# A tenth buffer for the first expert pieces, from a smaller descriptor scratch and dead tables, and two gathers and a selection moved from the fifth to the sixth group

## The chip, the core and the metric

The kernel runs on one core of a Trainium2 chip. The time is what the device takes for one execution, in microseconds (us), and less is better. The engines are TensorE (PE in the profile; PEld is its weight load), VectorE (DVE), ScalarE (ACT), GpSimd (POOL) and SyncE (SP), which here only issues DMAs. Each of them runs its own list of instructions in order and waits on semaphores for the others. DMAs that SP issues stand in one queue (q1, "hardware_dynamic"), those that POOL issues in another (q0, "software_dynamic"); both are served by the same 16 DMA engines.

## The reference, cut to what matters

One sequence of 256 tokens of width 1024 passes through two blocks. The first block is a mixer (an mLSTM and a latent attention, each with a branch projection, gated, merged and projected out) and then a mixture of experts; the second is a sparse attention mixer and a gated feed-forward layer with a short convolution. The change is in the mixture of experts and just ahead of it. Its core is this:

```python
in_grp = jnp.take_along_axis(e_logits, grp[:, None, None], axis=1)[:, 0]
top_p, top_e = lax.top_k(jax.nn.softmax(in_grp, axis=-1), TOP_K)
weights = p_grp[:, None] * top_p / jnp.sum(top_p, axis=-1, keepdims=True)
...
def run_block(args):
    xb, e, wb = args
    a = jax.nn.silu(xb @ w_gate[e]) * (xb @ w_up[e])
    return (a @ w_down[e]) * wb[:, None].astype(xb.dtype)
```

There are 32 experts. Each token is sent to two of them, chosen by a router (first one group of four, then the best two of its eight experts), and the two results are added with the router's weights. w_gate and w_up are 1024x256 and w_down is 256x1024 for each expert, all float32, so all experts together are 100.7 MB of weights.

## The kernel before, in words

**The groups.** The experts are taken four at a time, one on each quarter of the 128 partitions of the result, with room for 32 tokens each. Eight groups (numbers 0 to 7) cover the 32 experts once. Experts with more than 32 tokens get further blocks of 32: four "later" groups (numbers 8 to 11) with 15 blocks in all, whose experts are known only once the router is done. The order in which the groups are worked is `ORDER = [0, 1, 2, 8, 3, 9, 4, 5, 10, 6, 11, 7]`; `o` in the code is a position in it, `g` a group.

**The pieces.** The weights of a group of four experts come as six pieces of 2 MB, numbered 6g to 6g+5. Pieces 0 to 3 of a group hold gate and up columns and are used by `gate_up` (line 1347, 16 matmuls a piece), pieces 4 and 5 hold the down weights and are used by `down_rows` (line 1423, 16 matmuls a piece). SP issues the pieces in order (only piece 3, whose buffer comes free late, follows piece 7). For the first nine (`SLOTS = 9`) there are nine buffers made of whatever memory is free by then: four in `big`, one in `dring`, two in `ring`, one put together from `hT`, `gateb` and `pT`, and one from `xs` and `tail`. The list `FIRST` says which piece goes into which. From piece 9 on, the four buffers in `big` are used in turn (`RING = 4`), with one exception: piece `ONCE = SLOTS + RING = 13` goes into `dring`. SP issues a piece when the piece that was in its buffer before has been used; PE counts `s_used` up by one for each piece used. Beside this, `ring`, `dring`, `xs` and `tail` go over to the later groups.

**The later groups.** Their weights come in three parts each (two for gate and up, used by `later_gate_up`, line 1362; one for down, used by `later_down_rows`, line 1438). (8, 0) is the first part of group 8, (8, 2) its down part. POOL fetches each part with up to four indirect DMAs of 1 MB, one per block, whose row numbers come from the router (`later_piece`, line 2313). Blocks that no expert needs have row numbers out of range, and such rows are skipped. With these inputs one block is needed, group 8's first (all of POOL's queue moves 3.17 MB, three parts of one block); the DMAs of the other 14 are issued all the same. Parts alternate between two buffers: even numbers in `ring`, odd ones in `dring`, `xs` and `tail`. Part number 0, (8, 0), waits until the first pieces in `ring` are used (`s_used` at 8, that is piece 7). Part number 1, (8, 1), waits until `dring` is free, that is until piece 13 is used. Part number n from 2 on waits until part n-2 is used (`s_lused` at n-1). Where PE uses a part is written in three tables: `AFTER` (behind a group's first piece), `INSIDE` (behind its fourth) and `BEHIND` (after its down projection).

**Gathers and selections.** The tokens of two positions in `ORDER` (a pair q) are gathered by PE from the token rows with a 0/1 matrix that POOL builds (`select_pair`, lines 2292 and 2300): four `gather` calls per pair (line 1304, 8 matmuls each), each of which needs a PSUM bank that DVE and ACT must have emptied. Afterwards `selects` (lines 1314 and 1316) turns that matrix for the way back and takes out each row's weight; POOL may then build the next pair's matrix (it waits on `s_stw`). `scatter` (line 1374) adds the outputs of a position to the sum over all experts. `hidden_columns` (line 1396) turns the hidden activations ahead of the down projection. In group 4 the third and fourth gather of pair 4 and the selection of pair 4 stand between `hidden_columns` and the down projection.

**Ahead of the experts.** SP loads the mixer's last projections (`ba0`, `ba1`, `bm0`, `bm1`, `out0`, `out1`, 2 MB each in four quarters, line 640) as the quarters before them are used, and then the first pieces. `s_mt2` reaches 4 when the turned mLSTM output has been written, after the latent attention. `filler` (line 895) are matmuls on zeros whose result nobody reads.

## Time and profile before

| | us |
|---|---|
| median of 3 runs | 1025.64 |
| lowest and highest of the 3 | 1022.02, 1027.52 |
| the profiled execution's own time | 1023.9 |
| its span in the trace | 1022.1 |
| PE busy | 972.6 (95%) |
| PEld busy | 713.1 (70%) |
| DVE, ACT, POOL busy | 492.0, 385.7, 379.7 |

The span is cut into 40 slices of 25.6 us in the page. The experts run from about 350 us to about 571 us, slices 14 to 22. The page's DMA row has 9 (90% or more) in every slice from 13 to 20 and 8 in the next three; its GB/s row has 360 to 427 there. PE has 8 or 9 in each of these slices. So two resources are close to full in this stage, and a wait of one of them decides it only for stretches of a few microseconds. Times in the rows below are microseconds from the span's start. `[1.01 <-DMA big<-in_pieces_dram]` behind a row of the timeline says that the engine sat idle for 1.01 us before it and that this DMA ended the wait; "issue" says that nothing that the profile shows ended it.

### The profile page before, as it was taken

Reading aid. Unit: us, or ns where it says so; the run is one execution under the profiler, and the core shown is the slowest. Engines: PE = TensorE matmul, PEld = TensorE weight load, DVE = VectorE, ACT = ScalarE, POOL = GpSimd, SP = SyncE. Lnnn points to the kernel's source line nnn. Section 1 sums busy time; section 2 is a strip of 40 time slices with the busy share of each in tenths; the row PEclk is TensorE's granted clock in tenths of the full one; section 3 lists DMA queues with packets and bytes.
Section 4 is the critical chain, followed back from the end, with each engine's and each line's share of the span. In section 5 each row is a group of like instructions: output and inputs, shape, how many; then the busy total and the mean of one; then the engine's idle time right before and its main releaser. Section 6 shows DMA issues by size and latency. Waiting matters only on the chain.

```text
span 1022.1 us, 15203 instructions
## 1 busy us (share of the span) xinstructions
PE 972.6 (95%) x6120; PEld 713.1 (70%) x6120; DVE 492.0 (48%) x853; ACT 385.7 (38%) x617; POOL 379.7 (37%) x249
## 2 busy tenths in 40 slices
PE   7999999999999999898699999999999999999997
PEld 3887777777788544344243699777556789999996
DVE  1445358544244622213031603536665368777775
ACT  1633345445433321111020644544553254434342
POOL 0885747444783055453320499740002500000000
PEclk7999999999999999999799999999999999999999
DMA  9996955334469999999999888533224465454521
GB/s 377 345 414 266 372 172 158 87 100 124 144 208 427 360 425 423 416 398 370 407 407 414 310 321 255 156 93 103 86 80 144 165 268 195 176 204 165 205 82 41
DMA packets 49274, 252.08 MB, mean 247 GB/s; under 512 B 10432, under 2 KB 11072, under 8 KB 31424
## 3 DMA queue, kind: packets, MB, share of 16 engines
q1 hardware_dynamic: 42736, 248.10, 64.4%
q0 software_dynamic: 6480, 3.17, 1.1%
q8 instruction: 41, 0.67, 0.3%
q14 instruction: 17, 0.14, 0.0%
HBM read 294.22 MB, written 1.05 MB: 289 GB/s over the span
## 4 chain that ended last, share of the span: by engine, by line
PE 76%; DVE 7%; issue 6%; DMA 4%; ACT 3%; POOL 2%; DVEq 0%; SPq 0%; POOLq 0%; ACTq 0%
PE ps L885 33%; PE ps L1208 17%; PE ps L1347 3%; PE ps L781 2%; PE ps L1423 2%; PE ps L1362 2%; PE ps L1374 2%; PE ps L833 1%; PE ps L1304 1%; DMA tail<-in_experts_dram,xidx 1%; PE ps L1438 1%; DMA big<-in_pieces_dram 1%; DMA xs<-in_x_dram 1%; PE ps L895 1%; POOL sel L2292 1%
## 5 line engine op out<-in xcount | busy, mean ns | idle before, releaser
L2262 POOL TENSOR_TENSOR wl<-ring,wh 128x1024 fp32r<-128x1024 f32 (+5 forms) x132 | 289.3, 2211 | 228.9 <-ACT wh L1760 227.1
L1760 ACT ACTIVATE wh<-ring 128x1024 fp32r<-128x1024 f32 (+5 forms) x148 | 143.4, 983 | 132.1 <-PE ps L885 100.9
L885 PE MATMUL ps<-wh,hTh 128*128 128x512 f32 (+3 forms) x384 | 153.0, 398 | 1.3 <-DVE wl L3086 1.3
L885 PE MATMUL ps<-wl,hTh 128*128 128x512 f32 (+3 forms) x384 | 148.3, 386 | 0.0
L885 PE MATMUL ps<-wh,hTl 128*128 128x512 f32 (+3 forms) x352 | 136.7, 388 | 0.0
L1208 PE MATMUL ps<-hTs,wsp 128*128 128x256 f32 x1056 | 128.7, 284 | 0.5 <-DVE wsp L2922 0.5
L1208 PEld LDWEIGHTS ps<-hTs,wsp 128*128 128x128 f32 x1056 | 128.1, 192 | 1.5 <-DVE wsp L2922 0.7
L2250 POOL TENSOR_TENSOR small<-small 128x2 f32<-128x2 f32 (+2 forms) x7 | 5.3, 759 | 272.7 <-DVE small L3235 192.4
L885 PEld LDWEIGHTS ps<-wh,hTh 128*128 128x128 f32 x384 | 73.0, 190 | 22.7 <-issue 6.8
L885 PEld LDWEIGHTS ps<-wl,hTh 128*128 128x128 f32 x384 | 73.0, 190 | 13.5
L885 PEld LDWEIGHTS ps<-wh,hTl 128*128 128x128 f32 x352 | 66.8, 190 | 13.4
L1208 PE MATMUL ps<-wsp,aTs 128*128 128x512 f32 x264 | 61.7, 391 | 0.0
L1347 PE MATMUL ps<-big,xg 128*32 128x512 f32 x432 | 53.7, 605 | 7.3 <-DMA big<-in_pieces_dram 7.0
L885 PE MATMUL ps<-hTh,wh 128*128 128x256 f32 x208 | 58.1, 279 | 0.0
L885 PE MATMUL ps<-hTl,wh 128*128 128x256 f32 x208 | 58.0, 279 | 0.0
L885 PE MATMUL ps<-hTh,wl 128*128 128x256 f32 x208 | 57.6, 277 | 0.0
L1976 ACT ACTIVATE wsp<-ring 128x2048 fp32r<-128x2048 f32 x22 | 42.0, 1909 | 40.4 <-PE ps L1208 34.1
L1208 PEld LDWEIGHTS ps<-wsp,aTs 128*128 128x128 f32 x264 | 49.0, 188 | 9.7
L2922 DVE TENSOR_TENSOR wsp<-ring,wsp 128x2048 fp32r<-128x2048 f32 x22 | 50.3, 2285 | 9.5 <-ACT wsp L1976 9.5
L2292 POOL TENSOR_SCALAR sel<-cst,few 128x128 fp32r<-128x128 f32 x40 | 23.3, 596 | 58.6 <-PE ps L1316 58.6
L885 PEld LDWEIGHTS ps<-hTh,wh 128*128 128x128 f32 x208 | 39.1, 188 | 0.8 <-issue 0.8
L885 PEld LDWEIGHTS ps<-hTl,wh 128*128 128x128 f32 x208 | 39.1, 188 | 0.0
(481 smaller groups left out, 1637.3 us busy)
## 6 DMA issues: line engine op xcount, KB each, us to landing
big<-in_pieces_dram SPq DMA_DIRECT2D x42, 2048.0 KB
ring<-in_wa_dram SPq DMA_DIRECT2D x68, 512.0 KB, 3.9
big<-in_mod_dram SPq DMA_DIRECT2D x11, 2048.0 KB, 10.4
ring<-in_ffn_dram SPq DMA_DIRECT2D x11, 2048.0 KB, 9.1
ring<-in_wb_dram SPq DMA_DIRECT2D x40, 512.0 KB, 3.9
dring<-in_ffn_dram SPq DMA_DIRECT2D x11, 1024.0 KB, 4.9
ring<-in_wb_dram SPq DMA_DIRECT2D x12, 384.0 KB, 5.7
dring<-in_pieces_dram SPq DMA_DIRECT2D x2, 2048.0 KB, 21.4
```

The costliest lines, as they stand in the source:

```text
L781: mm = pe.matmul(ps[32 * q:32 * q + 32, 6, :], condw[:, c, :], mtile[n][:, c, :], start=(c < 4), stop=(c >= 4), skip_group_check=True)
L885: mm = pe.matmul(out, x[i], y[j], start=(p, c, k) == (0, 0, 0), stop=(c, k) == (KD - 1, 2), skip_group_check=True)
L1208: mm = pe.matmul(out, w[a], x[b], start=start and n == 0, stop=stop and n == 2, skip_group_check=skip)
L1347: mm = pe.matmul(ps[b * BS:(b + 1) * BS, 4, :], xg[q % 2][:, c, at:at + BS], slot_part(s, b)[:, cc * 512:(cc + 1) * 512], start=(c == 0), ...
L1362: mm = pe.matmul(ps[b * BS:(b + 1) * BS, 5, :], xg[q % 2][:, c, at:at + BS], later_slot(later_number(g, k), b)[:, cc * 512:(cc + 1) * 512] ...
L1374: mm = pe.matmul(ps[:, 2 * t + n, :], selT[:, (o // 2) % 2, o % 2, t * P:(t + 1) * P], x[:, n * 512:(n + 1) * 512], start=False, stop=Fals ...
L1423: mm = pe.matmul(ps[b * BS:(b + 1) * BS, 6 + n, :], aT[:, f, b * BS:(b + 1) * BS], slot_part(s, b)[:, n * 512:(n + 1) * 512], start=(f == ...
L1760: nc.scalar.activation(quarter(name, q, "high"), quarter(name, q, "raw"), ACT.Copy).then_inc(s_qh, 1)
L1976: nc.scalar.activation(wsp[:, 0 if last else m, 0, :], src, ACT.Copy).then_inc(s_hi[m], 1)
L2262: nc.gpsimd.tensor_tensor(quarter(name, q, "low"), quarter(name, q, "raw"), quarter(name, q, "high"), ALU.subtract).then_inc(s_ql, 1)
L2292: ins = nc.gpsimd.tensor_scalar(sel12[:, k, t, h * P:(h + 1) * P], const("iota"), gsp[:, k, t, g:g + 1], None, ALU.is_equal)
L2922: V.tensor_tensor(wsp[:, dst, 1, :], src, wsp[:, dst, 0, :], ALU.subtract).then_inc(s_lo[m], 1)
```

## The change

There is one more buffer for first pieces, number 9: three blocks of new memory (`tenth`, 12 KB a partition) and a fourth in the tables `cos`, `sin`, `chunk` and `tri`, which nobody reads after the latent attention. The memory comes from a descriptor scratch of 4096 bytes a partition in place of the default of 16384. To make the tables adjoin, `tri` is moved behind `chunk` and its bfloat16 copy is made earlier, in memory of its own; the zeros for `filler` become 480 columns wide.

Piece 0 goes into the new buffer and is issued between `bm0` and `bm1` once `s_mt2` is at 4. The other first pieces each move up by one place, so that ten pieces are loaded ahead of the ring. With `SLOTS` at 10, `ONCE` becomes 14: piece 14 is the one that goes into `dring`, part (8, 1) therefore waits for piece 14, and part (8, 0) waits for `s_used` at 9, that is piece 8. On PE part (8, 0) moves from inside group 2 to behind group 1. The third and fourth gather of pair 4 move from group 4's end to behind the second and third piece of group 5, and the selection of pair 4 moves from group 4 to group 5. On POOL the matrix of pair 5, which waits for that selection, moves behind parts (10, 1) and (10, 2).

PE at the end of group 1 and the start of group 2, before (`_66` is the second buffer of gathered tokens; 32x512 rows are pieces or parts, 128x256 rows gathers):

```order
L1423 MATMUL ps<-big,aT 32x512 [waits s_piece2]
L1423 MATMUL ps<-big,aT 32x512 x7
L1347 MATMUL ps<-big,xg_66 32x512 [waits s_xa,s_piece3]
L1347 MATMUL ps<-big,xg_66 32x512 x7
L1347 MATMUL ps<-dring,xg_66 32x512 [waits s_xv,s_piece4]
L1347 MATMUL ps<-dring,xg_66 32x512 x7
```

and now:

```order
L1430 MATMUL ps<-big,aT 32x512 [waits s_piece1]
L1430 MATMUL ps<-big,aT 32x512 x7
L1369 MATMUL ps<-ring,xg_66 32x512 [waits s_xv,s_xa,s_later0]
L1369 MATMUL ps<-ring,xg_66 32x512 x15
L1354 MATMUL ps<-big,xg_66 32x512 [waits s_xa,s_piece2]
L1354 MATMUL ps<-big,xg_66 32x512 x7
```

Part (8, 0), in `ring` and with its wait on `s_later0`, has moved ahead of all of group 2.

POOL from part (9, 2) on, before (dring, xs and tail rows are odd parts, ring rows even ones):

```order
L2313 DMA dring<-in_experts_dram,xidx 128x2048 [waits s_lused]
L2313 DMA dring<-in_experts_dram,xidx 128x2048
L2313 DMA xs<-in_experts_dram,xidx 128x2048
L2313 DMA tail<-in_experts_dram,xidx 128x2048
L2313 DMA ring<-in_experts_dram,xidx 128x2048 [waits s_lused]
L2313 DMA ring<-in_experts_dram,xidx 128x2048 x3
L2292 TENSOR_SCALAR sel_81<-cst,few 128x128 [waits s_stw]
L2292 TENSOR_SCALAR sel_81<-cst,few 128x128 x7
L2300 TENSOR_TENSOR sel<-sel_81 128x512 [waits s_ga2,c_pool]
L2313 DMA dring<-in_experts_dram,xidx 128x2048 [waits s_lused]
```

and now from part (10, 0) on:

```order
L2320 DMA ring<-in_experts_dram,xidx 128x2048 [waits s_lused]
L2320 DMA ring<-in_experts_dram,xidx 128x2048 x3
L2320 DMA dring<-in_experts_dram,xidx 128x2048 [waits s_lused]
L2320 DMA dring<-in_experts_dram,xidx 128x2048
L2320 DMA xs<-in_experts_dram,xidx 128x2048
L2320 DMA tail<-in_experts_dram,xidx 128x2048
L2320 DMA ring<-in_experts_dram,xidx 128x2048 [waits s_lused]
L2320 DMA ring<-in_experts_dram,xidx 128x2048 x3
L2299 TENSOR_SCALAR sel_81<-cst,few 128x128 [waits s_stw]
L2299 TENSOR_SCALAR sel_81<-cst,few 128x128 x7
L2307 TENSOR_TENSOR sel<-sel_81 128x512 [waits s_ga2,c_pool]
```

The matrix of pair 5 (sel) no longer stands ahead of part (10, 1), the second group of dring rows.

The diff, without most of its context:

```diff
@@ -51,16 +51,16 @@
 NPIECE = 6
-SLOTS, RING = 9, 4
-FIRST = [0, 1, 2, 7, 3, 4, 5, 6, 8]
+SLOTS, RING = 10, 4
+FIRST = [9, 0, 1, 7, 2, 3, 4, 5, 6, 8]
-INSIDE = {2: (8, 0), 3: (9, 0), 4: (9, 2), 5: (10, 1), 6: (11, 0), 7: (11, 2)}
+INSIDE = {3: (9, 0), 4: (9, 2), 5: (10, 1), 6: (11, 0), 7: (11, 2)}
-BEHIND = {2: (8, 1)}
+BEHIND = {1: (8, 0), 2: (8, 1)}
-SELECTS = {0: 0, 1: 1, 2: 2, 4: 3, 6: 4, 9: 5}
+SELECTS = {0: 0, 1: 1, 2: 2, 4: 3, 7: 4, 9: 5}
@@ -75,7 +75,7 @@
 CONST, NCONST = columns([
-    ("ident", P), ("ones", P), ("tri", P), ("cos", T), ("sin", T), ("chunk", SPAN), ("causal", SPAN),
+    ("ident", P), ("ones", P), ("cos", T), ("sin", T), ("chunk", SPAN), ("tri", P), ("causal", SPAN),
@@ -189,9 +189,11 @@
         pT = sb("pT", 3, SPAN)
-        zero = sb("zero", 512, dt=BF16)
+        zero = sb("zero", 480, dt=BF16)
+        halves16 = sb("halves16", 2, P, dt=BF16)
+        tenth = sb("tenth", 3, PIECE // QUAD)
@@ -286,6 +288,8 @@
                 return xs[:, b, :] if b < 2 else tail[:, b - 2, :]
+            if s == 9:
+                return tenth[:, b, :] if b < 3 else cst[:, CONST0:CONST0 + PIECE // QUAD]
...
@@ -420,8 +426,7 @@
         assert wh1_at + 4 * 1792 <= cst_at + 4 * NCONST
-        tri16 = at("tri16", spare_at + 4 * 1024, P, dt=BF16)[:, :]
-        ones16 = at("ones16", spare_at + 4 * (1024 + P // 2), P, dt=BF16)[:, :]
+        tri16, ones16 = halves16[:, 0, :], halves16[:, 1, :]
@@ -456,7 +461,7 @@
         s_lg, s_re, s_rx, s_diff = (sem(n) for n in ("s_lg", "s_re", "s_rx", "s_diff"))
-        s_piece = [sem(f"s_piece{n}") for n in range(SLOTS)]
+        s_piece = [sem(f"s_piece{n}") for n in range(SLOTS - 1)] + s_mt[3:]
@@ -667,10 +672,6 @@
             mod_tile(11)
-            for name, _, _ in LOADS[8:]:
-                load(name, wa)
-
-
@@ -678,6 +679,8 @@
                     sp.wait_ge(s_used, slot_before(n) + 1)
+                elif s == 9:
+                    sp.wait_ge(s_mt2, KD // 2)
@@ -690,7 +693,7 @@
                 w = PIECE // 2
-                if s == 7:
+                if s in (7, 9):
@@ -701,7 +704,11 @@
                                  pieces[n].rearrange("h p n -> p h n")).then_inc(s_piece[s], 16)
-            for n in (0, 1, 2, 4, 5, 6, 7, 3, 8):
+            for name, _, _ in LOADS[8:]:
+                load(name, wa)
+                if name == "bm0":
+                    expert_piece(0)
+            for n in (1, 2, 4, 5, 6, 7, 8, 3, 9):
...
@@ -1324,7 +1331,7 @@
                 s = slot(n)
-                first = 48 if s == 7 else 32 if s == 8 else 16
+                first = {7: 48, 8: 32, 9: 16 * mod_count(3) + 48}.get(s, 16)
@@ -1481,6 +1488,8 @@
                         early_gather(q, k - 1)
+                    if g == 5 and k in (1, 2):
+                        early_gather(4, k + 1)
@@ -1491,8 +1500,6 @@
                     hidden_columns(o)
-                    early_gather(q, 2)
-                    early_gather(q, 3)
@@ -2056,6 +2063,8 @@
                     gathered(q, 0, 6)
+                if g == 5:
+                    gathered(4, 2, 6)
@@ -2070,8 +2079,6 @@
                     outputs_high(o - 1)
-                if g == 4:
-                    gathered(q, 2, 6)
@@ -2304,9 +2311,9 @@
                 if n == 0:
-                    pool.wait_ge(s_used, FIRST.index(6) + 1)
+                    pool.wait_ge(s_used, max(FIRST.index(5), FIRST.index(6)) + 1)
-                    pool.wait_ge(s_used, max(SLOTS, ONCE + 1))
+                    pool.wait_ge(s_used, ONCE + 1)
@@ -2327,9 +2334,9 @@
             later_piece(10, 0)
-            select_pair(5)
+            select_pair(5)
@@ -2531,6 +2538,8 @@
             link.n += 1
+            link.later(V.tensor_copy(tri16, const("tri")))
+            link.later(V.tensor_copy(ones16, const("ones")))
@@ -2713,8 +2722,6 @@
             part_mean(4)
-            link.later(V.tensor_copy(tri16, const("tri")))
-            link.later(V.tensor_copy(ones16, const("ones")))
@@ -2893,6 +2900,8 @@
                     gathered(q, 1, 7)
+                if g == 5:
+                    gathered(4, 3, 7)
@@ -2900,7 +2909,7 @@
                     outputs_low(o - 1)
-                if q:
+                if q and g != 4:
@@ -3394,7 +3403,7 @@
               "rows": np.ascontiguousarray(rows), "mod": mod, "wa": wa, "experts": experts, "pieces": pieces, "wb": wb, "ffn": ffn}
-    nc = bacc.Bacc("TRN2", target_bir_lowering=False, num_devices=1)
+    nc = bacc.Bacc("TRN2", target_bir_lowering=False, num_devices=1, dynamic_dma_scratch_size=4096)
```

## Rows read from the trace of the kernel before

**Rows 1.** Stretches: bounds, us; PE, PEld, DVE, ACT, POOL busy; PEclk, DMA share, GB/s.
```profile
344.00:350.00 6.00, 4.85 (x26) 2.90 (x28) 4.01 (x15) 1.19 (x3) 0.00 (x0) 1.00 0.56 184
...
484.00:510.00 26.00, 17.50 (x125) 5.51 (x118) 1.69 (x4) 1.04 (x3) 9.71 (x10) 0.80 1.02 421
...
520.00:560.00 40.00, 39.59 (x295) 17.46 (x290) 10.18 (x18) 6.70 (x13) 6.10 (x6) 1.00 1.02 424
```

**Rows 2.** Chain of waits, 345 to 520 us: start us, us, what.
```profile
365.32 3.43 PE ps L1347 x32
368.76 1.14 PE ps L1304 x8
369.90 1.85 PE ps L1347 x16
...
382.50 10.20 DMA big<-in_pieces_dram
...
396.75 3.57 PE ps L1362 x32
...
476.23 4.67 POOL sel L2292 x8
...
486.41 13.14 DMA tail<-in_experts_dram,xidx
```

**Rows 3.** Timeline of PE, groups 2 and 3: start us, us, operation.
```profile
383.95 1.93 PE L1347 MATMUL ps<-big,xg 128*32 128x512 f32 x16
...
392.74 1.92 PE L1347 MATMUL ps<-big,xg 128*32 128x512 f32 x16 [1.01 <-DMA big<-in_pieces_dram]
...
407.64 0.63 PE L1362 MATMUL ps<-dring,xg 128*32 128x512 f32 x2
...
412.61 1.92 PE L1347 MATMUL ps<-big,xg 128*32 128x512 f32 x16 [1.33 <-DMA big<-in_pieces_dram]
...
420.87 5.34 PE L1438 MATMUL ps<-ring,aT 128*32 128x512 f32 x32 [3.45 <-issue]
...
426.00 1.93 PE L1347 MATMUL ps<-big,xg 128*32 128x512 f32 x16
```

**Rows 4.** Waits of ACT, 262 to 303 us: total us, times, longest.
```profile
ACT wh L1760 <- PE ps L885: 28.7, 16, 3.3
```

**Rows 5.** Timeline of SP: the issue of piece 10.
```profile
354.73 0.38 SPq L701 DMA_DIRECT2D big<-in_pieces_dram  x1
```

**Rows 6.** Timeline of POOL: first DMA of (8, 0) and of (8, 1).
```profile
369.81 1.26 POOL L2313 DMA_INDIRECT ring<-in_experts_dram,xidx  x1 [2.87 <-issue]
...
388.42 1.09 POOL L2313 DMA_INDIRECT dring<-in_experts_dram,xidx  x1 [2.16 <-PE ps L1347]
```

**Rows 7.** Both DMA queues, 380 to 385 us: packets, MB, share.
```profile
q1 hardware_dynamic: 272, 2.10, 99.1%
q0 software_dynamic: 271, 0.00, 3.1%
```

**Rows 8.** POOL's queue, 374 to 389 and 393 to 406 us.
```profile
q0 software_dynamic: 576, 1.05, 18.2%
...
q0 software_dynamic: 571, 1.04, 20.8%
```

**Rows 9.** Timeline of PE, groups 4, 5 and 7.
```profile
470.94 0.39 PE L1304 MATMUL ps<-sel,hnh 128*128 128x256 f32 x1 [1.03 <-DVE olt L2860]
...
476.53 3.64 PE L1423 MATMUL ps<-big,aT 128*32 128x512 f32 x32 [0.41 <-ACT selT L2025]
...
479.96 0.63 PE L1347 MATMUL ps<-big,xg 128*32 128x512 f32 x2
...
492.38 2.80 PE L1347 MATMUL ps<-big,xg 128*32 128x512 f32 x16 [3.62 <-DMA big<-in_pieces_dram]
...
499.59 1.07 PE L1362 MATMUL ps<-dring,xg 128*32 128x512 f32 x2 [4.41 <-DMA tail<-in_experts_dram,xidx]
...
554.12 1.92 PE L1347 MATMUL ps<-big,xg 128*32 128x512 f32 x16
```

More of the change, by code:

```diff
@@ L303, in slot_tile @@
                 return ring[:, (NLAST + s - 5) % 2, 0:PIECE]
+            if s == 9:
+                return tenth[:, 0:2, :].rearrange("p t n -> p (t n)")
             if s == 8:
@@ L894, in filler @@
                 for _ in range(n):
-                    pe.matmul(ps[:, b, :], zero[:, 0:P], zero[:, :], start=True, stop=True, skip_group_check=True)
+                    pe.matmul(ps[:, b, 0:480], zero[:, 0:P], zero[:, :], start=True, stop=True, skip_group_check=True)
             pe.wait_ge(s_zero, 1)
```

## The prediction, made before the changed kernel was run

> **What bounds the kernel now.** I read the stretches first, then the chain of waits, then the timelines of PE, SP and POOL and the DMA queues where the change acts. In the expert stage two resources are nearly full: from 520 to 560 us PE is busy 39.6 of 40 us and the DMA share is 1.02 at 424 GB/s; from 484 to 510 us PE is busy only 17.5 of 26 us at a mean granted clock of 0.80, while DMA stays at 1.02 [rows 1]. A 2 MB piece (2.097 MB) takes 4.95 us at 424 GB/s. The DMA engines have one early hole, 344 to 350 us, share 0.56 [rows 1]: all first buffers are full and the experts haven't started. The chain leaves PE for 10.20 us of a piece's DMA at 382.50, and later passes through POOL's matrix at 476.23 and 13.14 us of an indirect DMA at 486.41 [rows 2]. PE's waits on pieces are 1.01 us at 392.74, 1.33 at 412.61 and 3.62 at 492.38; those at 420.87 (3.45, shown as "issue", just where the part in `ring` must have landed) and 499.59 (4.41) are for later parts [rows 3, 9]. So there are three bounds that take turns: the stream of pieces, POOL's queue of parts, and PE. A buffer more helps the first alone; I have to see what it does to the second.
>
> **The tenth buffer.** Piece 0's 2 MB leave the stretch after 302 us and go beside the mixer's last projections. ACT there waits on PE's matmuls only (28.7 us in 16 waits) and on no DMA [rows 4], so I cost piece 0 at nothing; if its 4.95 us of DMA delayed `bm1` past its use, it would cost up to that. The gain is a stream 4.95 us ahead. But the first ring piece now waits for piece 1, not piece 0: piece 10 was issued at 354.73 [rows 5], a gather and a piece (1.14 + 1.85 [rows 2]) after piece 9, so 2.99 us of the lead are idle DMA. Net lead: 1.95 us.
>
> **Part (8, 0).** It now waits for piece 8, a gather and a piece later than piece 7, so its first DMA moves from 369.81 [rows 6] to 372.80. Its 576 packets filled 374 to 389 us [rows 8]. In 380 to 385 us POOL's queue got 271 packets through and SP's 272 [rows 7]: one each in turn, though POOL's rows were out of range and moved nothing. So a part of four blocks takes 10.6 us (576 packets at 54 a us) while pieces flow, and 15 when one block has data, however little it moves. The Trainium skill's page DMA: Bandwidth & Descriptors, section Queues, rings and completion order, says the engines go round-robin between queue rows a packet at a time; by that rule alone (8, 0) costs its upper bound below, unless the piece queue is empty. The trace agrees with it (271 against 272).
> So (8, 0) would end near 391.6, and PE sees a part some 1.9 us after its last packet (419 to 420.87, an estimate from where the packets of (8, 2) stop): 393.5. Before, PE came to it at 396.75. Now it stands behind group 1, where PE arrives at 383.95 [rows 3]: a wait of up to 9.5 us that wasn't there. What shortens it: piece 15 can't be issued before piece 10 is used, at about 382.5 [rows 2], and pieces 10 to 14 plus 1.05 MB of real rows (2.5 us) keep the queue busy from about 355.7 for 27.2 us, to 382.9. Then POOL's packets pass alone, for perhaps a microsecond. Bounds 2 and 9.5 us; I take 5, in the middle. PE starts (8, 0) at 388.9 and, at 3.57 us [rows 2], group 2 at 392.5 in place of 383.95.
>
> **Part (8, 1).** It waits for piece 14 in place of 13. Piece 14 is used two pieces (3.43), a gather and a piece after group 2's start, at 392.5 + 6.4 = 398.9; 0.9 us later the first DMA is issued, at 399.8 against 388.42 [rows 6]. Before, PE used the part at 407.64 [rows 3], 19.2 us after its issue, with 571 packets between 393 and 406 [rows 8]. Now: 399.8 + 19.2 = 419.0. PE arrives sooner: from group 2's start to (8, 1) it took 407.64 - 383.95 = 23.7 us, less (8, 0) with 3.57 and the wait of 1.01, so 19.1: 411.6. **A new wait of 7.4 us.** This is the step I trust most, since it needs only the order of POOL's waits and one issue-to-use time. Bounds: 2 us, if an empty piece queue helps it, and 10.
>
> **Part (8, 2).** From (8, 1)'s start to (8, 2)'s end PE took 426.00 - 407.64 = 18.4 us, of which waits are 1.33 and 3.45 and 1.7 is matmuls at a lower clock (5.34 us for 32 against 3.64 in row 476.53) [rows 3, 9]. The rest is 11.9: 419.0 + 11.9 = 430.9 without any wait. (8, 2)'s packets come 13 us behind (8, 1)'s and would be in time for 432.3, where PE needs them at 427.3: up to 5.0, less if the queue runs dry, since piece 22 can't be issued before piece 18 is used. I take 2, and 1.7 for matmuls after the long wait at the half clock, as after the wait at 420.87. So (8, 2) ends at 434.6: **8.6 us later than 426.00.**
>
> **Group 4.** Two gathers, the wait of 1.03 us ahead of them and a selection leave the stretch from about 469.9 to 476.53 [rows 9]. That is 1.03, two gathers at 1.14 and about 1.3, 4.6 us, the upper bound. But scatter needs three copies of group 9's outputs by DVE and ACT, the first of which is the one the 1.03 us waited for, and the gathers covered the other two; at something over 1 us a copy I take 1.8, with 0 as the lower bound: **-1.8**.
>
> **Groups 5 to 7.** The gathers go where PE waited 3.62 us, and POOL no longer builds pair 5's matrix (4.67 us, started 476.23 [rows 2]) ahead of (10, 1), whose wait of 4.41 us at 499.59 goes, with 0.9 us of slow matmuls (2.80 against 1.92). That makes 8.9 us on PE. But the piece stream is late next: piece 33 is used 492.38 - 479.96 = 12.4 us after group 4's end, and twelve more pieces at 4.95 follow, 59.4: piece 45 at 71.8 us, where it was 554.12 - 479.96 = 74.2 [rows 9]. PE's own work from piece 33 on is 554.12 - 492.38 = 61.7, less 4.41 and 0.9, plus an estimated 1.3 for the moved selection, 57.7 us against the stream's 59.4, so the stream sets it: **-2.4**. After piece 45 nothing changes.
>
> **Fillers.** 32 columns fewer, 13 ns a matmul at the full clock; only the 20 between the last pieces could be on the path: -0.3. The copies of `tri` and `ones` and the 64 KB that change DMA: nothing, DVE is at 48% on the page.
>
> **Sum.** 8.6 - 1.8 - 2.4 - 0.3 = +4.1 us on the profiled execution's 1023.9 (span 1022.1 and 1.8 around it): 1028.0. That execution lies 1.7 us below the median of 1025.64, so I predict 1025.6 + 4.1 = 1029.7, slower by 0.4%. The lead of 1.95 us from the tenth buffer isn't in the sum: once PE waits at (8, 1), the ring of four is full anyway.
>
> **Rival 1, the parts at full price (slower).** The piece queue never runs dry under the parts. Then (8, 0) costs 9.5 (4.5 more) and (8, 2) costs 5.0 (3.0 more): 1029.7 + 7.5 = 1037.2. For it: POOL's packets kept to one in turn for as long as pieces flowed [rows 7]. Against it: SP's queue is only four pieces deep and PE stands still. It decides from where (8, 0) is used later than 391 us.
>
> **Rival 2, the lead wins (faster).** Parts slip through in the holes that the waits make: (8, 0) costs 2 and (8, 1) about the same, and both are made up before 426 by the waits of 1.01, 1.33 and 3.45 that go. What stays is the lead of 1.95, the 1.8, the 2.4 and 0.3: 1025.6 - 6.4 = 1019.2. For it: the share of 0.56 at 344 us shows that the stream could start earlier, and PE's waits on pieces are real. Against it: (8, 1)'s issue depends on piece 14, which nothing brings forward.
>
> **Rival 3, no difference.** The stream of pieces has the same length and the ring is four deep either way; a delay of PE near 410 us is absorbed by the 3.62 and 4.41 near 495. Time 1025.6. The waits near 495 add up to enough (8.0 us), but the stream bound above leaves only 2.4 of them. Whether the smaller scratch slows POOL the trace of before can't show; its DMA rows wait on PE or on nothing that the profile shows [rows 6]. If POOL had to wait for room at every part, the time would be rival 1's, and it is in that chance.
>
> **Chances and range.** The forecast 0.43, rival 1 0.20, rival 2 0.25, rival 3 0.12. About 0.5% (5.1 us, from 1020.5 to 1030.8) is what a measurement of this kernel can tell from no change. The forecast's own range is 1026 to 1033, so 0.4 of it lies above 1030.8: slower 0.17 + 0.20 = 0.37. Faster is 0.8 of rival 2: 0.20. The same: the rest, 0.43. The range over the cases, with about a tenth left out on either side, is 1019 to 1036.
>
> **What would show it.** In the profile after: PE idle ahead of the first part behind group 1 (near 384 us, 2 to 9 us) and, longer, ahead of the part behind group 2 (near 411 us, 5 to 10 us), both ended by an indirect DMA; POOL's first `dring` DMA near 400 in place of 388; a granted clock below 1 just behind; group 5's fourth piece with a wait under 2 us, and none for the part behind it; DMA share near 1 from 490 to 560. I am wrong if PE runs through behind group 2 without a wait, or if group 3's first piece starts before 415 us. The step most likely to be mis-sized is the wait for (8, 0).

## The result, and the profile after

The changed kernel takes 1029.97 us (median of 9 runs, 1027.0 to 1032.36) against 1023.5 us (9 runs, 1019.75 to 1027.52) for the kernel before on the same chip: ratio 1.0069, 95% interval 1.0051 to 1.0087, so slower by 0.7%. The profiled execution has a span of 1028.9 us, 6.8 more than before. The difference arises in the expert stage. Its first expert matmul starts 1.46 us earlier (348.29 against 349.75), its last gate and up piece (piece 45) 6.75 us later. (On the page of the kernel before, the DMA row has its 9 up to slice 21, and PE's row has a 6, not 8 or 9, in slice 19, about 486 to 511 us, where the waits of 3.62 and 4.41 us lie.)

PE's timeline of the changed kernel, groups 1 to 3 (start us, us, operation; L1354, L1369, L1430, L1445 are L1347, L1362, L1423, L1438 of before), answers to [rows 3]:

```profile
384.75 5.34 PE L1369 MATMUL ps<-ring,xg 128*32 128x512 f32 x32 [2.03 <-DMA ring<-in_experts_dram,xidx]
...
394.59 1.92 PE L1354 MATMUL ps<-dring,xg 128*32 128x512 f32 x16
...
416.57 1.07 PE L1369 MATMUL ps<-dring,xg 128*32 128x512 f32 x2 [7.65 <-DMA tail<-in_experts_dram,xidx]
...
421.58 1.89 PE L1354 MATMUL ps<-big,xg 128*32 128x512 f32 x16
...
428.72 4.23 PE L1445 MATMUL ps<-ring,aT 128*32 128x512 f32 x32
432.77 1.89 PE L1354 MATMUL ps<-big,xg 128*32 128x512 f32 x16
```

PE stands 2.03 us for (8, 0), then works on it for 5.34 us in place of 3.57, and stands 7.65 us for (8, 1). Piece 19 starts at 432.77, where it was 426.00. POOL's timeline and its queue say why (8, 1) is late:

```profile
371.36 1.26 POOL L2320 DMA_INDIRECT ring<-in_experts_dram,xidx  x1 [5.86 <-issue]
...
397.34 1.09 POOL L2320 DMA_INDIRECT dring<-in_experts_dram,xidx  x1 [12.55 <-PE ps L1354]
```

POOL stood 12.55 us until PE had used piece 14 (the `dring` row at 394.59), and PE got the part 19.2 us after its issue, exactly as before (388.42 to 407.64 [rows 3, 6]).

What follows is new. Stretches 426 to 438 us (the columns of [rows 1]; the seventh value is the granted clock, then DMA share and GB/s), the kernel before and the changed one:

```profile
426.00:438.00 12.00, 12.00 (x104) 5.96 (x100) 5.34 (x8) 3.48 (x6) 4.12 (x4) 1.00 1.02 417
```

```profile
426.00:438.00 12.00, 12.00 (x83) 4.72 (x82) 3.17 (x3) 2.08 (x3) 4.57 (x6) 0.86 0.57 203
...
474.00:484.00 10.00, 7.79 (x38) 3.54 (x29) 2.51 (x2) 1.43 (x2) 3.56 (x3) 0.69 1.02 412
...
480.00:490.00 10.00, 9.07 (x60) 3.95 (x64) 2.51 (x2) 1.28 (x2) 4.58 (x4) 0.83 0.74 265
```

The DMA share of 0.57 in place of 1.02 is a hole of 12 x 0.45 / 1.02 = 5.3 us in the stream. The ring of four was full and piece 23 may only be issued once PE has used piece 19, which PE did 6.8 us late. So PE's wait has become lost time of the other full resource. It is the largest hole, not the only one: the share is 0.83 from 450 to 460 us and 0.74 from 480 to 490, where the kernel before has 1.02 and 0.97.

Groups 4 to 7 of the changed kernel, against [rows 9]:

```profile
473.01 0.62 PE L1445 MATMUL ps<-dring,aT 128*32 128x512 f32 x2 [2.72 <-issue]
...
480.93 1.84 PE L1381 MATMUL ps<-oh__67,selT 128*128 128x512 f32 x4 [2.21 <-ACT oh__67 L2039]
482.57 1.91 PE L1381 MATMUL ps<-ol__69,selT 128*128 128x512 f32 x4
484.41 3.69 PE L1430 MATMUL ps<-big,aT 128*32 128x512 f32 x32
487.93 1.89 PE L1354 MATMUL ps<-big,xg 128*32 128x512 f32 x16
...
499.04 1.92 PE L1354 MATMUL ps<-big,xg 128*32 128x512 f32 x16
500.78 0.60 PE L1369 MATMUL ps<-dring,xg 128*32 128x512 f32 x2
...
515.34 3.57 PE L1354 MATMUL ps<-big,xg 128*32 128x512 f32 x16 [3.07 <-DMA big<-in_pieces_dram]
...
560.87 1.92 PE L1354 MATMUL ps<-big,xg 128*32 128x512 f32 x16 [0.30 <-DMA big<-in_pieces_dram]
```

The waits of 3.62 and 4.41 us near 495 are gone: PE is 8.0 us late at 487.93 and only 1.2 at (10, 1) (500.78 against 499.59). But that isn't kept. The pieces are late too, PE waits for them (3.07 us at 515.34) and is again 6.75 us late at the last one. At 515.34 it is 4.0 us late (511.36 before), and the rest comes piece by piece behind it. A bound that PE had caught up with was not the one that counts.

### The profile page after: what moved, and what is told of

The parts are those of the page before. It is cut to its first block, busy times and chain, and to the rows that moved or that the text cites. A ratio compares the mean times of both kernels' runs of the same rounds, so it can differ in the third digit from the quotient of the medians.

```text
span 1028.9 us, 15205 instructions
## 1 busy us (share of the span) xinstructions
PE 975.4 (95%) x6120; PEld 712.1 (69%) x6120; DVE 495.3 (48%) x853; ACT 385.5 (37%) x617; POOL 380.7 (37%) x249
## 3 DMA queue, kind: packets, MB, share of 16 engines
q0 software_dynamic: 6480, 3.17, 1.1%
## 4 chain that ended last, share of the span: by engine, by line
PE 76%; DMA 8%; DVE 8%; issue 3%; ACT 3%; POOL 1%; DVEq 0%; SPq 0%; POOLq 0%; ACTq 0%
PE ps L892 32%; PE ps L1215 17%; DMA big<-in_pieces_dram 4%; PE ps L1354 4%; PE ps L1369 2%; PE ps L788 2%; PE ps L1381 2%; PE ps L1430 2%; PE ps L1445 2%; PE ps L1311 2%; DMA tail<-in_experts_dram,xidx 1%; PE ps L840 1%; DMA xs<-in_x_dram 1%; DMA ring<-in_experts_dram,xidx 1%; PE ps L1119 1%
## 5 line engine op out<-in xcount | busy, mean ns | idle before, releaser
L1215 PE MATMUL ps<-wsp,aTs 128*128 128x512 f32 x264 | 61.7, 390 | 0.0
L1354 PE MATMUL ps<-big,xg 128*32 128x512 f32 x400 | 49.4, 614 | 6.4 <-DMA big<-in_pieces_dram 6.4
L892 PEld LDWEIGHTS ps<-hTh,wl 128*128 128x128 f32 x208 | 39.6, 190 | 0.0
```

Source lines behind the costliest of these rows:

```text
L892: mm = pe.matmul(out, x[i], y[j], start=(p, c, k) == (0, 0, 0), stop=(c, k) == (KD - 1, 2), skip_group_check=True)
L1215: mm = pe.matmul(out, w[a], x[b], start=start and n == 0, stop=stop and n == 2, skip_group_check=skip)
L1354: mm = pe.matmul(ps[b * BS:(b + 1) * BS, 4, :], xg[q % 2][:, c, at:at + BS], slot_part(s, b)[:, cc * 512:(cc + 1) * 512], start=(c == 0), ...
```

## The experiments

In the table, "stage" runs from PE's first expert matmul to the start of piece 45, in the profiled execution (before 204.4, changed 212.6). "Idle" is how long the DMA engines stood in it: over the 20 stretches of 10 us from 350 to 550 us, the sum of 10 x (1.02 - share), where 1.02 is the share of a full queue (before 4.7, changed 13.5; good to a few tenths). Ratios are against the kernel before, run beside each, with 95% intervals.

| kernel | median us | ratio | stage us | idle us |
|---|---|---|---|---|
| changed, (8, 0) inside group 2 | 1023.53 | 1.0014 (0.9994 to 1.0034) | 206.5 | 8.0 |
| before, small scratch | 1023.77 | 1.0012 (0.9997 to 1.0026) | 202.7 | 2.9 |
| before, moved gathers | 1020.44 | 0.9972 (0.9956 to 0.9988) | 202.0 | 3.5 |
| changed, gathers not moved | 1030.5 | 1.0054 (1.0031 to 1.0078) | 212.1 | 13.7 |
| changed, piece 13 in dring | 1026.59 | 1.0030 (1.0013 to 1.0047) | 208.9 | 9.8 |
| the first and the fifth together | 1020.31 | 0.9979 (0.9963 to 0.9996) | 202.9 | 4.4 |
| changed, one DMA a part | 1015.76 | 0.9925 (0.9911 to 0.9940) | 198.1 | 3.4 |
| before, one DMA a part | 1014.64 | 0.9919 (0.9904 to 0.9934) | 197.8 | 2.6 |
| before, moved gathers, piece 12 in dring | 1019.99 | 0.9968 (0.9949 to 0.9988) | 201.9 | 3.0 |
| before, (8, 0) behind group 1 | 1031.77 | 1.0080 (1.0059 to 1.0102) | 211.5 | 10.4 |
| changed, (8, 0) inside, piece 12 in dring | 1023.56 | 1.0012 (0.9990 to 1.0033) | 203.7 | 5.5 |
| sixth, big at its old position | 1019.74 | 0.9969 (0.9951 to 0.9986) | 201.2 | 5.5 |

Stage less idle is 198 to 201 us in every row with all DMAs and in both kernels of the comparison, except the last row (196). So what sets these kernels apart is for the most part how long the stream of pieces stood. In the two rows with one DMA a part it is 195.

**(8, 0) back inside group 2.**

```diff
-INSIDE = {3: (9, 0), 4: (9, 2), ...
+INSIDE = {2: (8, 0), 3: (9, 0), 4: (9, 2), ...
-BEHIND = {1: (8, 0), 2: (8, 1)}
+BEHIND = {2: (8, 1)}
```

> The changed kernel, with part (8, 0) back inside group 2 and all else as changed. Theory (the order of POOL's waits): the loss is the wait for part (8, 1), 7.65 us at 416.57, which is issued only when piece 14 is used. With (8, 0) behind piece 15 again, PE no longer stands 2.03 us and no longer works 5.34 us (1.7 of it for the half clock) ahead of group 2, so pieces 12 to 14 are used some 7 to 9 us earlier and POOL issues (8, 1) near 389 in place of 397.34, while PE arrives at it only some 3.7 us sooner. The wait for (8, 1) falls to 2 to 5 us, group 3's piece 18 starts at 416 to 418 in place of 421.58, and of the 6.5 us that the change costs 2 to 5 go: 1025 to 1028. Rival (the late dring alone): the place of (8, 0) doesn't matter, since the wait is for POOL's queue of packets; time within 1 us of the changed kernel, 1029 to 1031. Rival (late parts don't decide, the stream does): also 1029 to 1031, with less wait at (8, 1) and more at pieces behind.

1023.53 us: all of the loss but 0.1% goes, a little more than the theory gave. PE's wait for (8, 1) falls from 7.65 to

```profile
410.26 0.62 PE L1369 MATMUL ps<-dring,xg 128*32 128x512 f32 x2 [4.20 <-DMA tail<-in_experts_dram,xidx]
```

and the DMA share from 426 to 438 us rises from 0.57 to 0.78; piece 19 starts at 429.20, where it was 432.77. Both rivals (1029 to 1031) are out.

**The small scratch alone.**

```diff
-    nc = bacc.Bacc("TRN2", target_bir_lowering=False, num_devices=1)
+    nc = bacc.Bacc("TRN2", target_bir_lowering=False, num_devices=1, dynamic_dma_scratch_size=4096)
```

> The kernel before with a descriptor scratch of 4096 bytes a partition in place of the default, nothing else. Theory: POOL doesn't lack room for descriptors, so the time is that of the kernel before within 0.2% (1021.5 to 1025.5), and the issue of (8, 0) to its first packet stays near 4.4 us. Rival (the smaller scratch slows POOL's indirect DMAs): parts (8, 1), (8, 2) and (10, 1), on which PE waits already, come later, 3 to 8 us slower, 1027 to 1032, and this alone would be the loss of the change.

1023.77 us, ratio 1.0012 with an interval up to 1.0026. A loss of 3 us or more by the scratch is excluded, one of 1 to 2 us isn't; the stage of its profile is no longer than before.

**The moved gathers alone** (`SELECTS`, the two `early_gather` and `gathered`, and `select_pair(5)` as in the change, on the kernel before).

> The kernel before with only the third and fourth gather of pair 4 and its selection moved to group 5, and POOL's matrix of pair 5 behind (10, 1) and (10, 2); nine buffers and part (8, 0) inside group 2 as before. Theory: group 4 ends 1 to 3 us earlier, the wait of 4.41 us for (10, 1) goes, but the stream of pieces is late next, so the wait of 3.62 us on a piece grows; in all 1 to 4 us faster than before, 1019.5 to 1022.5, and the loss of the whole change stands apart from this part. Rival (the moved gathers cost in groups 5 and 6 what they give in group 4): the same as before or up to 3 us slower, 1023.5 to 1026.5.

1020.44 us, as the theory said: this half of the change is worth 2.8 us (1.2 to 4.5) by itself. Its timeline shows where it came from and where not:

```profile
472.81 1.17 PE L1374 MATMUL ps<-oh__67,selT 128*128 128x512 f32 x4 [2.21 <-ACT oh__67 L2032]
473.98 2.07 PE L1374 MATMUL ps<-ol__69,selT 128*128 128x512 f32 x4
475.98 4.25 PE L1423 MATMUL ps<-big,aT 128*32 128x512 f32 x32
...
480.06 1.89 PE L1347 MATMUL ps<-big,xg 128*32 128x512 f32 x16
...
491.46 1.92 PE L1347 MATMUL ps<-big,xg 128*32 128x512 f32 x16 [0.23 <-DMA big<-in_pieces_dram]
```

Group 4 ends where it did (480.06 against 479.96): without the gathers, `scatter` waits 2.21 us for the third copy, and the matmuls behind are slow. The gain lies behind it: 480.06 to piece 45 at 551.68 is 71.6 us, where before had 74.2.

**The rest of the change alone** (the changed kernel with gathers, selection and matrix where they were).

> The changed kernel without the moved gathers, selection and matrix: the tenth buffer, the smaller scratch, the tables, (8, 0) behind group 1. Theory: the waits for (8, 0) (2 us) and (8, 1) (7.7 us) are those of the changed kernel, PE is 8 us late at the end of group 4 as there, and of what groups 5 to 7 recover only the stream's own slack is left: 1030 to 1035, slower than the changed kernel by 0 to 4 us, since PE works two gathers and a selection ahead of group 4's end. Rival (the moved gathers are the loss): 1023 to 1027, near the kernel before.

1030.5 us: the loss is all in this half. In its company the moved gathers gain nothing that can be measured. Of the theory's two waits only one is there: PE stands 2.22 us for (8, 0), but only 0.43 for (8, 1). It had stood 2.07 and 1.63 us for DVE and ACT just before, and had run the down projection at a low clock (5.34 us), and all this lay under the same landing of (8, 1): issued at 397.61, used at 415.67. Piece 19 starts at 433.52, as late as in the changed kernel. So it is the time at which a part lands that counts; how PE fills the time until then doesn't.

**Piece 13 in place of 14 in dring.**

```diff
-ONCE = SLOTS + RING
+ONCE = SLOTS + RING - 1
```

> The changed kernel with piece 13 instead of piece 14 in dring (14 then goes into the ring), and nothing else: part (8, 1) waits for piece 13, which PE uses a gather and a piece (3.1 us) sooner. Theory (the order of POOL's waits makes PE late, and PE being late lets the stream run dry at piece 23, which waits for the use of piece 19): (8, 1) is issued near 394.3 in place of 397.34, PE's wait for it falls from 7.65 to between 4 and 5.5 us, piece 19 is used some 3 us earlier, the stream's hole of 6.3 us falls to about 3, and the same 2 to 4 us show at the last piece and in the time: 1026 to 1028. Rival (the hole is only beside the loss, which comes from the wait for (8, 0) and slow matmuls behind it): 1029 to 1031.

1026.59 us, 3.4 less than the changed kernel (ratios 1.0030 and 1.0069), as the theory said. But the way there was another. (8, 1) was issued at 395.54 and used 2.4 us sooner (414.20), with a wait of only 1.57 us, since two waits for copies of gathered rows (1.25 and 1.30 us) had held PE before it. Then the wait came back one part later:

```profile
414.20 0.62 PE L1369 MATMUL ps<-dring,xg 128*32 128x512 f32 x2 [1.57 <-DMA tail<-in_experts_dram,xidx]
...
427.62 2.79 PE L1445 MATMUL ps<-ring,aT 128*32 128x512 f32 x12 [3.65 <-issue]
...
480.00:490.00 10.00, 10.00 (x86) 3.29 (x88) 2.83 (x3) 1.06 (x1) 3.17 (x3) 1.00 1.00 371
```

Piece 19 starts at 432.65, where the changed kernel has 432.77, and the hole is nearly the same: from 424 to 444 us the DMA share is 0.76, against 0.73. The expectation of a hole of about 3 us was wrong. What goes is the second hole, at 480 to 490 us (last row: share 1.00 in place of 0.74). In the changed kernel PE had waited 2.72 us for (9, 2), ran at a low clock behind it and began piece 28 at 484.41; here it waits 1.08 us, keeps the full clock and begins it at 481.51, and piece 32 may only be issued once piece 28 is used. Why (9, 2) was less late here isn't shown.

**Both cures together.**

> Both cures in the changed kernel: part (8, 0) inside group 2 and piece 13 in dring. Theory: (8, 1) is issued near 388 and lands near 406, PE's wait for it falls from 4.20 (with (8, 0) inside group 2 alone) to 0 to 2 us, the hole in the stream from 3.7 to under 1 us, the last piece comes 2 to 4 us sooner: 1019.5 to 1022, faster than before by 1 to 4 us and the fastest of the ten-buffer kernels. Rival (the waits for (8, 2) and for outputs take the place of that for (8, 1)): 1023 to 1025, no better than (8, 0) inside group 2 alone.

1020.31 us, faster than before. It is also 3 us less than with (8, 0) inside group 2 alone (1023.53; the intervals of the two ratios just touch), which is what waiting for piece 14 in place of 13 costs there. POOL issues (8, 1) at 387.53, PE waits 1.18 us for it, and the stream has no hole from 426 to 438:

```profile
426.00:438.00 12.00, 12.00 (x104) 5.93 (x100) 5.24 (x8) 3.49 (x6) 4.13 (x4) 1.00 1.02 390
```

**One indirect DMA a part, in the changed kernel and in the kernel before.** They leave out the fetch of every group's second to fourth block, 11 of the 14 that no expert needs with these inputs.

```diff
-                for b in range(later_blocks(g)):
+                for b in range(1):
                     pool.indirect_dma_start(
```

> The changed kernel with one indirect DMA for each later part in place of one per block; the blocks left out are those that no expert needs with these inputs, 33 of 45 DMAs, so the real rows moved are the same 3.17 MB. Theory (rows out of range cost a packet each and a turn in the round robin): (8, 1), issued near 397, lands at about 407 in place of 415, PE meets no wait over 1 us for it or for (8, 2), the stream runs dry nowhere in the middle of the stage, and the time is 1017 to 1022, 8 to 13 us under the changed kernel. Rival (out-of-range rows cost nothing, only the real megabyte and the late issue count): PE still waits 5 to 8 us for (8, 1), 1027 to 1030.

> The kernel before with one indirect DMA for each later part, the same blocks left out. Theory: the waits of 3.45 us for (8, 2) and 4.41 us for (10, 1) go, but the stream of pieces sets the end, which is relieved only of the packets of skipped rows: 1018 to 1022. Against the changed kernel with the same edit this shows what the tenth buffer and the moved gathers are worth when parts are cheap: that one should be 0 to 3 us faster than this. Rival (the parts were hidden in the kernel before): 1022.5 to 1024.5.

1015.76 and 1014.64 us: 14 and 8 us less than with all DMAs, more than expected of both. The bytes that POOL fetches are the same 3.15 to 3.17 MB; only packets of skipped rows went (6480 to 1728), and with them 33 DMAs that POOL has to issue, some 1.3 us apart (371.36, 372.93, 374.22, 375.52 in the changed kernel). In neither profile does PE wait for a part any more. So the skipped blocks are most of the price of a part; whether by their packets' turns or by the time that POOL takes to issue them no run separates. A part's four DMAs are issued in 5 us and its packets take over 10 (576 at 54 a us), which speaks for the turns. And once parts are cheap, the tenth buffer with the moved gathers is not faster than nine buffers (expected: 0 to 3 us faster).

**Nine buffers with the moved gathers and an earlier (8, 1).**

```diff
-ONCE = SLOTS + RING
+ONCE = SLOTS + RING - 1
```

> The kernel before (nine buffers) with the moved gathers, selection and matrix, and with piece 12 instead of piece 13 in dring, so that (8, 1) waits for piece 12. Theory (the tenth buffer is worth nothing by itself; order at POOL and the moved gathers are): (8, 1) is issued near 385.5 in place of 388.42, the wait of 3.45 us for (8, 2) falls to 0.5 to 2, and the time is that of the ten-buffer kernel with both cures, 1020.31, or up to 2.5 us below: 1018 to 1020.5. Rival (the tenth buffer is worth its 2 us of lead once its parts are in time): 1021 to 1023, slower than that kernel.

1019.99 us. Nine buffers give what ten give (0.9968 against 0.9979); the rival's 1021 to 1023 isn't met, though the intervals overlap. The wait for (8, 2) fell only from 3.45 to 2.96 us.

**The suspected cause put into the kernel before.**

```diff
-INSIDE = {2: (8, 0), 3: (9, 0), 4: (9, 2), ...
+INSIDE = {3: (9, 0), 4: (9, 2), ...
-BEHIND = {2: (8, 1)}
+BEHIND = {1: (8, 0), 2: (8, 1)}
```

> The kernel before (nine buffers, all else as before) with part (8, 0) behind group 1 and nothing else. Its packets end at 388.6 there and PE sees them near 390.5. Theory (where PE meets (8, 0) decides when piece 13 is used, and with that (8, 1)'s issue): PE waits about 6.5 us at 384 for (8, 0), starts group 2 at 394 to 396 in place of 383.95, (8, 1) is issued near 400 and waited for 5 to 9 us, the stream has a hole of 5 to 8 us, and the time is 1028 to 1033: the whole loss of the change without its tenth buffer. Rival (the tenth buffer, which lets (8, 1) wait for a piece more, is needed for the loss): 1024 to 1027, since the ring of four makes up a wait for (8, 0) alone.

1031.77 us, slower by 0.8%: the whole loss, with nine buffers and (8, 1) waiting for piece 13 as before. The chain of the theory is there, the waits split otherwise (5.02 and 3.17), and from 430 to 442 us the DMA share is 0.77:

```profile
390.37 1.08 PE L1362 MATMUL ps<-ring,xg 128*32 128x512 f32 x4 [5.02 <-DMA ring<-in_experts_dram,xidx]
...
418.38 0.62 PE L1362 MATMUL ps<-dring,xg 128*32 128x512 f32 x2 [3.17 <-DMA tail<-in_experts_dram,xidx]
```

```profile
400.65 1.09 POOL L2313 DMA_INDIRECT dring<-in_experts_dram,xidx  x1 [13.24 <-PE ps L1347]
```

**Piece 12 in dring, with (8, 0) inside** (`ONCE = SLOTS + RING - 2`).

> The ten-buffer kernel with (8, 0) inside group 2 and piece 12 (not 13, not 14) in dring. Theory: (8, 1) is issued near 386 in place of 387.53, its wait of 1.18 us goes and that for (8, 2) falls from 3.64 to 2 to 3; piece 12 now waits for piece 6 in place of 4, some 3.5 us of idle stream near 364, while ten buffers are full, which nobody feels: 1018 to 1020.5. Rival (that idle stream is the lead that the tenth buffer gave and is missed later, since pieces set the pace from 440 on): 1021 to 1024.

1023.56 us: the rival holds by the time. The idle stream is there (363 to 373 us, share 0.83 against 1.01 in the kernel with both cures) and is felt 30 us later:

```profile
394.05 2.34 PE L1354 MATMUL ps<-big,xg 128*32 128x512 f32 x12 [2.66 <-DMA big<-in_pieces_dram]
```

Its stage is only 0.8 us longer in the one profiled execution, against 3 us in the medians (the intervals of the two ratios overlap a little), so the size stays open.

**big at its old position.** The table of waits didn't explain why ten buffers weren't faster. The pace of the stream did: packets of the pieces' queue from 530 to 555 us, before and changed.

```profile
q1 hardware_dynamic: 1366, 10.54, 99.8%
```

```profile
q1 hardware_dynamic: 1335, 10.31, 99.5%
```

A piece of 2.097 MB takes 4.97 us in the first (25 x 2.097 / 10.54) and 5.09 in the second, at the same full queue. Part of the difference is POOL's: it has 847 packets in this stretch of the changed kernel, 613 before. The new tiles ahead of `big` had moved its start in each partition to 448 bytes past a multiple of 512, where it was on one.

```diff
-        zero = sb("zero", 480, dt=BF16)
-        halves16 = sb("halves16", 2, P, dt=BF16)
         big_at = here()
         big = sb("big", BIG)
+        zero = sb("zero", 480, dt=BF16)
+        halves16 = sb("halves16", 2, P, dt=BF16)
```

> The ten-buffer kernel with both cures ((8, 0) inside group 2, piece 13 in dring), and big placed ahead of zero and halves16, so that it begins at a multiple of 512 bytes in each partition as in the kernel before; in the changed kernel it begins 448 bytes past one. What this tells apart: all seven ten-buffer kernels so far took 5.02 to 5.06 us a piece where the stream sets the pace, all six nine-buffer ones 4.93 to 4.99, packets of 8 KB about 2% longer. Theory A (where big begins costs the packets their 2%): 530 to 555 us shows about 1366 packets of the pieces' queue in place of some 1335, 4.97 us a piece, 1.5 to 3.5 us off the stage, and a time of 1017 to 1019. Theory B (the tenth buffer itself or the smaller scratch slows the stream): pace 5.04 to 5.06 as before, and 1019.5 to 1021.5 us.

The same stretch with both cures alone, and with `big` back as well; POOL has 433 and 432 packets in it:

```profile
q1 hardware_dynamic: 1352, 10.43, 100.5%
```

```profile
q1 hardware_dynamic: 1371, 10.58, 100.0%
```

Theory A holds for the pace: 4.96 us a piece in place of 5.03, with ten buffers and the small scratch in both. The stage is 1.7 us shorter than with both cures alone; the time, 1019.74 us, is the lowest of the versions that do all the work, but above the 1017 to 1019 expected. Against 1020.31 the runs show no gain (0.9969 and 0.9979, with overlapping intervals), so what the pace is worth in time stays open.

## Why the prediction was right, and where its sizes were off

The forecast was 1025.6 + 4.1 = 1029.7 and the measured 1029.97, but partly by luck: the kernel before came down to 1023.5 with more runs, so the change costs 6.5 us, not 4.1. In the profiles PE is 6.8 us late at piece 19, 8.0 behind group 4 and 6.75 at piece 45; the forecast had 8.6, 6.8 and 4.4 there. So a first term that was too large hid a part of what the two others lacked.

**(8, 0)** was predicted to cost a wait of 5 us (2 to 9.5) and cost 2.03, plus 1.8 for matmuls at the half clock behind the wait, which I had counted only behind (8, 2). The reason given for less than 9.5 is in the trace: SP's queue ran empty and POOL's packets went alone.

**(8, 1)** was the step I trusted most. Issue predicted 399.8, measured 397.34; issue to use 19.2 and 19.2; wait 7.4 and 7.65. The runs show the place of (8, 0) as the cause from both sides: (8, 0) back inside group 2 takes all but 0.1% of the loss away, and its place alone brings the whole loss into the kernel before. The late (8, 1) is the link between: PE's delay at (8, 0) delays piece 14 and so (8, 1), as the forecast had it. With (8, 0) inside, the later gate is worth another 3 us (1023.53 to 1020.31, waits 4.20 and 1.18). In the changed kernel itself, one piece less to wait for took half of the loss away but left piece 19 where it was, so that run doesn't bear on this link. Nor is the length of the wait the measure: where the gathers weren't moved it was 0.43 us with the same loss.

**(8, 2)** was to end 8.6 us late, and piece 19 starts 6.8 late (8.2 on the stage's own clock). It needed no wait. In place of that wait stand the slow matmuls of (8, 1) (5.0 us), 1.71 us ahead of `scatter` for a copy, and (8, 2)'s own slow matmuls (4.23 us in place of 3.64).

**Group 4**, -1.8, failed. Alone it moved nothing (480.06), and in the changed kernel PE is 8.0 us late behind it, 1.2 more than at piece 19. I had given `scatter` 1 us a copy; it waited 2.21 us for the last one, and `scatter` (3.5 us for 2.0) and others then ran at a low clock (0.69 from 474 to 484 us). Besides, (9, 2) was waited for 2.72 us, where before had 0.85. What an operation hides goes back on the path when it is moved.

**Groups 5 to 7**, -2.4 and -0.3: the bound was the right one. On the kernel before it is -2.5 (71.6 against 74.2). In the changed kernel it is -1.2 (560.87 - 487.93 = 72.9), and the term that was too small is "twelve more pieces at 4.95", 59.4 us: from piece 33 to piece 45 it was 61.8 (499.04 to 560.87). Of these 2.4 us some 0.9 belong to where `big` begins, which I had costed at nothing with the memory layout, `zero` and `halves16`: with both cures the same twelve take 61.7 us (490.08 to 551.77), with `big` back 60.8 (488.70 to 549.46). The rest isn't explained; with nine buffers and the moved gathers they took 60.2 (491.46 to 551.68), so 4.95 was too small there as well.

**The tenth buffer.** I left its lead of 1.95 us out of the sum, and that was right, though for more reasons than I gave: with both cures it is level with nine buffers even when `big` is back in place (0.9969 and 0.9968). What I did not see is where the loss becomes permanent. I followed PE and took the stream as a floor under its recovery. It is rather the clock of the stage: PE's delay of 6.8 us opened a hole of 5.3 us in it, and no later slack of PE's own can close that. From 350 to 550 us the DMA engines stood 8.8 us longer than before (13.5 against 4.7), and the stage is 8.2 us longer. Rival 3 ("a delay of PE near 410 us is absorbed by the 3.62 and 4.41 near 495") fell for this reason: absorbed it was, and given back from 515 us on.

## What to carry to other kernels

Where a stream with a ring of buffers is the pacemaker, judge a reordering by whether it opens a hole in the stream, not by the waits of the engine behind it: the waits can be made up, the hole can't. A buffer more changes which use every gate waits for: count them all. Here it brought nothing even with the gates put right, and cost 3 us through the gate of (8, 1). And see where the unchanged buffers end up in memory when new tiles are put ahead of them: it changed the pace here by 1.4%, though no gain in time was shown.

## What the runs showed of the hardware

**Skipped rows have the price of a turn.** With both queues full, POOL's packets go one for one with the pieces' [rows 7], though they move nothing. It is the part that pays: the pieces' packets still have 99.1% of the engines there, the skipped ones 3.1%, some 9 ns each. Where the pieces' queue is empty, they pass at once. Both queues of the changed kernel, 380 to 385 and 382.2 to 382.5 us (packets, MB, share; in a stretch as short as a packet the share says little):

```profile
q1 hardware_dynamic: 215, 1.63, 88.7%
q0 software_dynamic: 467, 0.16, 12.6%
```

```profile
q1 hardware_dynamic: 24, 0.11, 237.8%
q0 software_dynamic: 233, 0.00, 43.9%
```

233 packets of skipped rows in 0.3 us, against 271 in 5 us. All 4752 that went with the skipped blocks are by the 9 ns an estimated 2.7 us of 16 engines; in the two kernels with one DMA a part, stage less idle is some 4 us below that of the kernels they come from. The Trainium skill's page DMA: Bandwidth & Descriptors, section Queues, rings and completion order, has the engines go round-robin between the rows that they have work for; both stretches agree with that.

**Where a destination begins changes its packets' cost.** In the pair that differs in nothing else, 1352 packets at a share of 100.5% against 1371 at 100.0%: 1.9% more engine time for each (25 x 16 x share / packets is 0.297 and 0.292 us). Only two positions were tried, so which multiple matters is open. The same page, section How a descriptor splits into AXI transactions, says that a descriptor not starting at a multiple of 256 bytes begins its first transaction at the boundary below. 448 bytes lie 192 past such a boundary, so by that rule an 8192-byte row costs an estimated (8192 + 192) / 8192, 2.3% more. The trace's 1.9% is close to it. The page puts the rule in terms of reading, and here it is the destination that begins off the boundary; the transactions themselves no trace shows.

**The half clock often follows a wait of PE.** After the wait of 7.65 us the 32 matmuls of (8, 1) take 5.0 us (416.57 to 421.58), where those of (8, 0) took 3.57 before [rows 2]; from 386 to 388 us, behind the 2.03 us for (8, 0), the granted clock is 0.50, the lower of the two levels (1.2 of 2.4 GHz), and from 474 to 484 us it is 0.69. Such a part costs its wait and up to 1.8 us more. It isn't a rule by the length of the wait: in the kernel with the gathers not moved, (8, 0) was waited for 2.22 us, and its 32 matmuls took 3.64 us at a granted clock of 1.00 (386 to 392 us).
